# Sums over later keys from rounded high and low parts, 384 columns at once

## The reference

```python
def one_block(args):
    qb, start = args
    z = jnp.einsum('bhqd,bhkd->bhqk', qb, k).astype(jnp.float32) * scale
    q_pos = start + jnp.arange(Q_BLOCK)
    mask = k_pos[None, :] < q_pos[:, None]
    log_beta = jax.nn.log_sigmoid(z)
    log_1m = jnp.where(mask, jax.nn.log_sigmoid(-z), 0.0)
    suffix = lax.cumsum(log_1m, axis=3, reverse=True) - log_1m
    a = jnp.where(mask, jnp.exp(log_beta + suffix), 0.0)
    return jnp.einsum('bhqk,bhkd->bhqd', a.astype(v.dtype), v)
```

## The kernel before

| chunk, d | step d+1 | step d+2 | step d+3 | step d+4 |
|---|---|---|---|---|
| 0, 23 | w | a, w | w | a, w |
| 1, 47 | a, w | a, w | w | a, w |
| 2, 71 | a, w | w | a, w | w |
| 3, 95 | w | a, w | a, w | w |

## Time and profile before

### The profile page before, as it was taken

How to read it: one execution, slowest core, us unless ns; L and a number is a source line. 1 busy time by engine, 2 the same in 40 slices (tenths; PEclk the granted TensorE clock), 3 DMA queues, 4 the chain that set the end, 5 groups by cost and what they waited for, 6 DMA issues and landing times.

```text
span 1951.6 us, 24848 instructions
## 1 busy us (share of the span) xinstructions
PE 1932.6 (99%) x9262; PEld 1618.0 (83%) x9262; DVE 1504.0 (77%) x2044; ACT 1014.2 (52%) x1477; POOL 125.4 (6%) x88
## 2 busy tenths in 40 slices
PE   9999999999999999999999999999999999999999
PEld 7888888888888888888888888888887888888877
DVE  5786777777677777777776568888898688888986
ACT  5545455445535444444435455566646455666553
POOL 1221233000000000000000000001100000010000
PEclk9999999999999999999999999999999999999999
DMA  7787867789888888988887646655565465555554
GB/s 254 240 270 236 284 223 249 255 278 309 277 304 278 286 302 276 302 293 293 292 282 252 194 155 175 186 166 158 155 205 181 144 190 164 177 165 156 195 181 142
DMA packets 225947, 445.10 MB, mean 228 GB/s; under 512 B 15795, under 2 KB 57189, under 8 KB 225571
## 3 DMA queue, kind: packets, MB, share of 16 engines
q1 hardware_dynamic: 225443, 443.08, 70.0%
q10 hardware_dynamic: 384, 0.44, 0.1%
HBM read 441.34 MB, written 2.11 MB: 227 GB/s over the span
## 4 chain that ended last, share of the span: by engine, by line
PE 81%; DVE 10%; ACT 4%; POOL 3%; issue 2%; DMA 0%; ACTq 0%; DVEq 0%; POOLq 0%
PE P L704 25%; PE P L706 25%; PE P L705 24%; DVE WL L1062 3%; PE P L467 2%; DVE CA L1059 2%; POOL ST L1464 1%; ACT WH L1033 1%; PE P L499 1%; DVE FB L1359 1%; POOL QK L1490 1%; PE P L576 1%; DVE X L1423 1%; PE P L586 1%; PE P L587 1%
## 5 line engine op out<-in xcount | busy, mean ns | idle before, releaser
L1062 DVE TENSOR_TENSOR WL<-RAW,WH 128x1024 fp32r<-128x1024 f32 x648 | 790.2, 1224 | 310.4 <-ACT WH L1033 309.3
L1033 ACT ACTIVATE WH<-RAW 128x1024 fp32r<-128x1024 f32 x648 | 670.5, 1045 | 565.1 <-PE P L706 434.6
L704 PE MATMUL P<-WH,AH 128*128 128x512 f32 (+1 forms) x1536 | 604.7, 394 | 4.5 <-DVE WL L1062 2.8
L706 PE MATMUL P<-WH,AL 128*128 128x512 f32 (+1 forms) x1536 | 594.7, 387 | 0.0
L705 PE MATMUL P<-WL,AH 128*128 128x512 f32 (+1 forms) x1536 | 593.4, 386 | 0.0
L704 PE MATMUL P<-WH,BH 128*128 128x512 f32 x896 | 353.0, 394 | 0.0
L706 PE MATMUL P<-WH,BL 128*128 128x512 f32 x896 | 349.2, 390 | 0.0
L705 PE MATMUL P<-WL,BH 128*128 128x512 f32 x896 | 348.6, 389 | 0.0
L704 PEld LDWEIGHTS P<-WH,AH 128*128 128x128 f32 x1536 | 288.9, 188 | 61.7 <-issue 4.0
L706 PEld LDWEIGHTS P<-WH,AL 128*128 128x128 f32 x1536 | 288.7, 188 | 59.1
L705 PEld LDWEIGHTS P<-WL,AH 128*128 128x128 f32 x1536 | 289.1, 188 | 54.6
(11 more groups left out here) (249 smaller groups left out, 1392.1 us busy)
## 6 DMA issues: line engine op xcount, KB each, us to landing
RAW<-in_ada_w_dram SPq DMA_DIRECT2D x192, 512.0 KB, 5.0
RAW<-in_mlp_w_in_dram SPq DMA_DIRECT2D x128, 512.0 KB, 4.7
RAW<-in_mlp_w_out_dram SPq DMA_DIRECT2D x128, 512.0 KB, 5.2
RAW<-in_sb_w_qkv_dram SPq DMA_DIRECT2D x96, 512.0 KB, 5.0
RAW<-in_w_in_dram SPq DMA_DIRECT2D x80, 512.0 KB, 4.1
RAW<-in_w_in_dram SPq DMA_DIRECT2D x128, 256.0 KB, 3.1
RAW<-in_w_out_dram SPq DMA_DIRECT2D x64, 512.0 KB, 3.8
RAW<-in_sb_w_o_dram SPq DMA_DIRECT2D x32, 512.0 KB, 5.4
```

The lines of the kernel that those rows point to most:

```text
L704: e.matmul(o, xh, wh, start=u.first and k == 0, stop=False)
L706: return e.matmul(o, xl, wh, start=False, stop=u.last and k == u.nk - 1)
L1033: e.activation(WH[:, n % NH, 0:size], RAW[:, i % NR, 0:size], ACT.Copy).then_inc(w_high, 1)
L1062: return e.tensor_tensor(o, x, h.bitcast(F32), ALU.subtract)
```

## The change

The softplus tile is split into a high part `TNH` (a rounded copy by ScalarE, in the place of `TL`) and a low part `TNL` (the rest, by VectorE, in the place of `TN`). TensorE multiplies the rounded triangles with both: two rounded matmuls of 384 columns and two of 128 columns a head. A new task `sb_high` stands at step d+3; `sb_sums` moves to d+4 and `sb_out` to d+5. ScalarE rounds the two constant matrices once, in the first `sb_high`. ScalarE's `sb_scores` waits for the sums of the chunk before, since `TL` is now read by them.

```diff
+        UNR = put("UNR", [128, 128], F32R, off=oTQ + 512)
+        NGR = put("NGR", [128, 128], F32R, off=oTQ + K)
...
+        TNH = put("TNH", [128, 4, 384], F32R, off=oS + 24 * K)
+        TNL = put("TNL", [128, 4, 384], F32R, off=oS + 36 * K)
...
-                        after[d + 3].append(("sb_sums", j, hp))
-                        after[d + 4].append(("sb_out", j, hp))
+                        after[d + 3].append(("sb_high", j, hp))
+                        after[d + 4].append(("sb_sums", j, hp))
+                        after[d + 5].append(("sb_out", j, hp))
...
-                    e.wait_ge(*tn_mask.at(j, h))
-                    e.matmul(pb[:, 0:128], UN, TN[:, h, 0:128], start=True, stop=True)
-                    e.matmul(pb[:, 128:256], UN, TN[:, h, 128:256], start=True, stop=False)
-                    e.matmul(pb[:, 128:256], NG, TN[:, h, 256:384], start=False, stop=True)
-                    m = e.matmul(pb[:, 256:384], UN, TN[:, h, 256:384], start=True, stop=True)
+                    e.wait_ge(*un_r.at(0))
+                    e.wait_ge(*tn_low.at(j, h))
+                    e.matmul(pb[:, 0:384], UNR[:, :], TNH[:, h, :], start=True, stop=False, skip_group_check=True)
+                    e.matmul(pb[:, 0:384], UNR[:, :], TNL[:, h, :], start=False, stop=False, skip_group_check=True)
+                    e.matmul(pb[:, 128:256], NGR[:, :], TNH[:, h, 256:384], start=False, stop=False, skip_group_check=True)
+                    m = e.matmul(pb[:, 128:256], NGR[:, :], TNL[:, h, 256:384], start=False, stop=True, skip_group_check=True)
...
-                        e.wait_ge(*T.emptied(("z", j - 1, h)))
+                        e.wait_ge(*T.ready(("sum", j - 1, h)))
...
+            def sb_high(j, hp):
+                if j == 0 and hp == 0:
+                    e.wait_ge(s_cst, 16)
+                    e.activation(UNR[:, :], UN, ACT.Copy)
+                    e.activation(NGR[:, :], NG, ACT.Copy).then_inc(*un_r.up(0))
+                for h in (2 * hp, 2 * hp + 1):
+                    e.wait_ge(*tn_mask.at(j, h))
+                    e.activation(TNH[:, h, :], TN[:, h, :], ACT.Copy).then_inc(*tn_high.up(j, h))
...
+            def sb_high(j, hp):
+                for h in (2 * hp, 2 * hp + 1):
+                    e.wait_ge(*tn_high.at(j, h))
+                    e.tensor_tensor(TNL[:, h, :], TN[:, h, :], TNH[:, h, :].bitcast(F32), ALU.subtract).then_inc(*tn_low.up(j, h))
```

More of the change, by code:

```diff
@@ L113, in build @@
         CS = put("CS", [128, 2, 2, 32])
+        oTQ = at[0]
         TQ = put("TQ", [128, 4, 2, 32])
         TK = put("TK", [128, 4, 2, 32])
+        UNR = put("UNR", [128, 128], F32R, off=oTQ + 512)
+        NGR = put("NGR", [128, 128], F32R, off=oTQ + K)
         CC = put("CC", [128, 16])
@@ L413, in build @@
         tally = lambda n: Tally(sem(n))
+        un_r, tn_high, tn_low = tally("sum_masks_rounded"), tally("sb_neg_high"), tally("sb_neg_low")
         cols, c_act, angle_d, angle_a = tally("columns"), tally("c_act"), tally("angle_vec"), tally("angle_sin")
@@ L429, in build @@
         p_high, x_done = tally("p_high"), tally("x_added")
-        tallies = [cols, c_act, angle_d, angle_a, sq_sum, ms, rstd, x_high, x_end, x_gated, h_diag, h_full, h_high, h_low, scl, qk_sq, qk_ms, qk_done, qk_red,
+        tallies = [un_r, tn_high, tn_low, cols, c_act, angle_d, angle_a, sq_sum, ms, rstd, x_high, x_end, x_gated, h_diag, h_full, h_high, h_low, scl, qk_sq, qk_ms, qk_done, qk_red,
                    lnexp, tn_mask, a_exp, a_mask, bh_high, hid_sq, hid_high, hid_low, pads, tabs, sig, lat_sq, lat_ms, lat_r, lat_high,
@@ L1035, in scalar_program @@
             tasks = dict(x_turn=x_turn, x_square=x_square, columns=columns, angles=angles, qk_evict=qk_evict, v_evict=v_evict, qk_turn=qk_turn,
-                         sb_scores=sb_scores, sb_sums=sb_sums, sb_out=sb_out, hid_evict=hid_evict, hid_turn=hid_turn, h_split=h_split, h_first=h_first, h_shift=h_shift, x_end_square=x_end_square, high=high,
+                         sb_scores=sb_scores, sb_high=sb_high, sb_sums=sb_sums, sb_out=sb_out, hid_evict=hid_evict, hid_turn=hid_turn, h_split=h_split, h_first=h_first, h_shift=h_shift, x_end_square=x_end_square, high=high,
                          z_evict=z_evict, glu=glu, lat_turn=lat_turn, q_evict=q_evict, k_evict=k_evict, k_scale=k_scale, att_turn=att_turn, att_scores=att_scores,
@@ L1423, in o_add @@
                     e.tensor_tensor(o, o, FB[:, t, :], ALU.add).then_inc(*(x_done if part else x_mid).up(l, c, t))
-            tasks = dict(x_turn=x_turn, x_add=x_add, rms=rms, rms_end=rms_end, x_end=x_end_, h_diag=h_diag_, h_first=h_first, columns=columns, taps=taps, ada_sum=ada_sum, qk_norm=qk_norm, sb_scores=sb_scores, sb_sums=sb_sums,
+            tasks = dict(x_turn=x_turn, x_add=x_add, rms=rms, rms_end=rms_end, x_end=x_end_, h_diag=h_diag_, h_first=h_first, columns=columns, taps=taps, ada_sum=ada_sum, qk_norm=qk_norm, sb_scores=sb_scores, sb_high=sb_high, sb_sums=sb_sums,
                          sb_out=sb_out, hid_turn=hid_turn, mod_scale=mod_scale, h_split=h_split, rms_part=rms_part, pads=pads_, rope_tables=rope_tables,
```

## The result

The changed kernel takes 1957.26 us (median of 16 runs, 1955.3 to 1958.3), the kernel before in the same comparison 1953.65 (16 runs, 1952.43 to 1956.22): a ratio of 1.0016, with a 95% interval of 1.0009 to 1.0023. Slower by 0.16%: clear of zero, and inside the 0.2% that the forecast took as the least a measurement can tell (the upper end of the interval is a little beyond it). The profiled executions differ by 1955.8 - 1951.6 = 4.2 us of span.

The account below looks back on a forecast made before the run. TensorE, busy 99% of the span, was taken as the bound. Blocks 0 to 3 at +2.1, +2.2, -0.3 and -0.7 sum to +3.3, taken as +3.2 on 1952.8: median 1956.0 us, 8-in-10 range 1951.0 to 1959.0.

Parts of the forecast that it names:

- The waits at the sums: TensorE's first sums matmul waits for VectorE's subtraction: 2.0, 2.9, 1.7 us in blocks 0 to 2, none in 3.
- VectorE starts the subtractions where it used to start the sums: On VectorE, the new subtractions begin at the old start of its sums, 99.10 in block 0.
- The chain from there to the outputs: VectorE's additions, then GpSimdE's masks: outputs end 4.8 us after additions start, or 6.7 with slowed masks.
- masks slowed in blocks 0 and 1: GpSimdE's four masks beside a VectorE modulation piece take 4.8 us in blocks 0 and 1, 2.8 in 2 and 3.
- Rival A: In the four blocks TensorE's gain goes through without waits: -4.1 to -7.7 us, time 1945.1 to 1948.7; chance 0.07.
- narrow rounded matmul: In TensorE's sums, 128 rounded columns taken as 0.223 us, lower bound 0.112; a head 0.79 or 0.57.
- rival C: TensorE's clock falls in the long waits at the sums: +0.9 to +3.2 us over forecast, 1956.9 to 1959.2; chance 0.23.
- TensorE's own bound: End of a block's outputs by TensorE: sums start plus four heads 3.18, unit 2.72, outputs 2.68; block 0 108.3.
- Rival B: Waits at the sums stay but masks aren't slowed in blocks 0 and 1: -0.3 to +2.2 us, 1952.5 to 1955.0; chance 0.20.

Follow-up runs that it names:

- x4: Changed kernel with VectorE making the weights' low part before the modulation piece in step d+4 of blocks 0 and 1; ratio 1.0005, 1954.29 us.
- x1: Changed kernel with the split into high and low parts one step earlier (d+2); ratio 1.0021, median 1957.17 us.
- x8: Changed kernel with its steps and added ScalarE and VectorE work, but float32 sums on the unsplit tile; ratio 1.0027, 1959.2 us.
- x7: Kernel before with sums moved to d+4 and outputs to d+5, float32 sums, no split; ratio 0.9991, 1951.75 us.
- x5: Changed kernel with the split at d+2, sums at d+4 and outputs at d+7; ratio 0.9965, 1946.48 us.
- x6: Kernel before with only its outputs moved from d+4 to d+5, float32 sums, no split; ratio 0.999, median 1951.99 us.
- x2: Changed kernel with the outputs one step later (d+6); ratio 1.0005, 1954.38 us.
- x3: Changed kernel with two spare 512-column float32 matmuls in the wait before the first sum of blocks 0 to 2; ratio 1.0016, 1956.16 us.

## Why the prediction was right, point by point

- **The waits at the sums.** Said 2.0, 2.9, 1.7 and none; measured 2.33, 2.81, 1.62 and none. The step "VectorE starts the subtractions where it used to start the sums" held (98.96 for 99.10 in block 0).
- **The chain from there to the outputs.** Additions said 3.1 us behind the subtractions, measured 3.01 in blocks 0 and 1; masks slowed in blocks 0 and 1 (3.80 and 4.89, said 4.8 for both), clean in 2 and 3 (2.80, 2.81). x4 shows the cause of the slow ones by taking it away. The Trainium skill (SBUF — State Buffer, section SBUF: two separate sides) says that an instruction of VectorE with two SBUF inputs and one of GpSimdE exclude each other; the 2.82 of x4 against 4.89 agree.
- **VectorE's added work, not the operand, is the loss.** x1 takes the wait at the sums away and keeps the loss; x8 has no such wait, and is 4.7 us or more slower than x7 with the same products on TensorE; x5, which covers the chain, turns the loss into a gain. Rival A (the gain goes through) needs just that cover, and its span of -4.1 to -7.7 holds x5's -6.2.
- **Mis-sized: the narrow rounded matmul.** I took 0.223 us. A head takes 0.58, not 0.79; less two of 384 columns at 0.174 that leaves 0.116 for each narrow one, my lower bound of 0.112. In the sum that is worth only what the forecast said of this choice, 0.8 us: +2.5, not +3.3. It shows in block 3, -1.5 for -0.7. The reason given for 0.223, that no row shows a narrow form keeping the pace, was a reason for a wide range, not for the end taken. The matmuls' own starts spread the price unevenly (183.15, 183.21, 183.32, then 0.23 to the next); the weight loads (PEld) of block 1 show it plainly. The loads behind the narrow matmuls follow after 0.11 us, those behind the wide ones after 0.17 to 0.18:

```profile
183.16 0.19 PEld L534 LDWEIGHTS P<-TNL,NGR 128*128 128x128 f32 x1
183.27 0.19 PEld L531 LDWEIGHTS P<-TNH,UNR 128*128 128x128 f32 x1
183.38 0.19 PEld L532 LDWEIGHTS P<-TNL,UNR 128*128 128x128 f32 x1
183.56 0.19 PEld L533 LDWEIGHTS P<-TNH,NGR 128*128 128x128 f32 x1
183.73 0.19 PEld L534 LDWEIGHTS P<-TNL,NGR 128*128 128x128 f32 x1
```

- **Mis-weighed: rival C.** The clock did fall, in block 0 of the profiled execution, for +1.7 us in that block. There TensorE's own bound was late: four heads 4.3 us and the unit behind them 3.9 instead of 2.3 and 2.8. By the mean clock and the times it fell in some 11 of 16 runs, where I gave it 0.23. I had held against this rival that here the wait comes from dense work; that did not protect the clock.
- **Luck in the number.** The median is nearly on the forecast because errors cancel: 0.8 too much for the matmuls and about 2 us for the clock in most runs, left out. The kernel before also came out 0.8 us higher in the comparison (1953.65) than the 1952.82 that the forecast started from. So the difference was forecast as +3.2 and measured as +3.6; the five runs with the highest mean clock, median 1955.49, are only 1.8 over 1953.65. They are picked by their clock, and so are also runs in which it held better at the start of the kernel; 1.8 is therefore no clean measure of the change without a fall.
- **Rival B** (masks not slowed) fell.

In block 1 a wait of 2.81 us left the clock whole, in block 2 one of 1.62 did; in x4 the same wait of block 2 was followed by a fall. The Trainium skill (TensorE: Matmul & The Clock Gate, section What's actually happening) says that idleness brings the engine to half rate, and that the place of a change differs from run to run. The runs agree with the second more than I had used; with the first only in part, since in x6 the clock fell without a wait ahead of it. What decides it in a single run stays open.

## What to carry to other kernels

A split into high and low parts moves work from TensorE to the engines that feed it. Where those run their lists in order and without gaps, find what the added work stands in front of and how many units of TensorE's own work lie between that and its consumer; with one unit of cover too few the saving turns into a wait, which an earlier operand only shifts to the next task. So move the consumer at the end of the chain first. Here the operand one step earlier gained nothing (x1), the outputs one step later won back 3.4 us of the 4.3 (x2), and only both, with two steps more for the outputs, made 0.16% slower into 0.35% faster (x5).

## What the runs showed of the hardware beyond that

- A rounded matmul of 128 columns with its own weight load costs a head of the sums 0.11 us, half of what a float32 one does (0.223), though it has a third of the columns of one that costs 0.17. The Trainium skill (TensorE: Matmul & The Clock Gate, section Back-to-back issue gap) gives some 81 ns for a 128-column matmul in a stream with its weight load; the 56 ns that the prediction took from it is its figure for a matmul by itself. The 0.11 measured here is above both, and agrees with the 107 ns for a weight load that the prediction cited as a floor.
- The length of a wait did not settle whether the clock fell, and with the same program its mean differs from run to run. Behind a wait at the sums it fell in block 0 of the changed kernel (2.33 us) and not in block 0 of x2 (2.62); in block 1 of x2 (2.81) and not in block 1 of the changed kernel or x4 (2.81); in block 2 of x4 (1.62) and not in block 2 of the changed kernel or x2 (1.62). In x6 it fell behind no wait at all. The falls measured here cost some 1.6 us (the changed kernel against x3, and x6).
- The wait of 1.99 us at the start is the same: behind it the granted clock was 0.62 from 10.0 to 14.5 us before, 0.62 in x3 and 0.67 in x1, but 1.00 after and in x4 and x5. Also, the first matmul that needs the loaded vector `VR` started at 5.84 us before, and at 6.57, 6.45 and 6.79 in x1, x3 and x8, where it waited 0.8 to 1.0 us for its load instead of 0.3. Both move what is behind them; the first mask of block 0 stood between 90.03 (x5) and 92.18 (x8). That is 2.2 us, a good part of the 3.8 over which the 16 runs of the kernel before spread, and it is why effects of 1 us are read from a point behind it. That these two are all of the spread is not shown.
